# The third mixer of a fused four-layer block, with its state-space groups started earlier

## The reference

```python
def odd_mixer(h, pos, w_in, lam_re, ..., q_norm, w_uq, kv_norm, w_ukv, w_out):
    u, c_q, c_kv, k_rope = split_cols(h @ w_in, ODD_SIZES)
    y_c = s5_group(u, ...)          # state space, 512 channels
    y_d = mla_group(c_q, c_kv, k_rope, pos, ...)   # latent attention, 8 heads
    return jnp.concatenate([y_c, y_d], axis=-1) @ w_out

def s5_group(u, ...):
    bu = jnp.einsum('bsgh,gph->bsgp', ug.astype(jnp.complex64), b_bar)
    _, state = lax.associative_scan(s5_combine, (a_el, bu), axis=1)
    y = jnp.real(jnp.einsum('bsgp,ghp->bsgh', state, cm)) + d_skip * ug
    y = jax.nn.gelu(y)
    return y * jax.nn.sigmoid(y @ w_glu + b_glu)

def mla_group(...):
    q = (rms_norm_2(c_q, q_norm) @ w_uq)     # nope and rope parts of the queries
    kv = (rms_norm_2(c_kv, kv_norm) @ w_ukv) # keys and values
    ...                                       # rope, causal softmax by blocks, values
```

## Time and profile before

| | us |
|---|---|
| median of 3 runs | 2521.75 (2520.43 to 2522.57) |
| the profiled execution | 2520.07 |
| its span in the trace | 2518.3 |
| PE busy | 2442.2 (97% of the span) |
| DVE busy | 1301.7 (52%) |
| POOL busy | 1059.2 (42%) |
| ACT busy | 866.6 (34%) |
| from the first matmul of the third mixer to its last | 1879.1 to 2139.0 |

### The profile page before, as it was taken

One profiled execution on the slowest core, in us unless ns is written; L12 is line 12 of the kernel. 1 busy time (PEld: TensorE's weight loads), 2 busy tenths in 40 slices (PEclk: granted clock), 3 DMA queues, 4 the chain that ended last, 5 costly groups with the idle time before them and its releaser, 6 DMA issues.

```text
span 2518.3 us, 30094 instructions
## 1 busy us (share of the span) xinstructions
PE 2442.2 (97%) x11662; PEld 1962.8 (78%) x11662; DVE 1301.7 (52%) x1928; ACT 866.6 (34%) x1360; POOL 1059.2 (42%) x830
## 2 busy tenths in 40 slices
PE   8999999999999999999999999999999889999998
PEld 6877767888888888876777778888888657788886
DVE  6336687533533321494767754686126855533301
ACT  4453346222322222334445533222224453322221
POOL 4323344644544444353322245554454223544442
PEclk9999999999999999999999999999999989999999
DMA  4212122232323233222222223323231112222232
GB/s 148 68 59 78 55 78 90 95 101 92 105 93 100 94 96 96 93 85 66 74 67 75 72 75 107 98 94 98 92 100 55 28 34 81 91 92 101 91 98 80
DMA packets 65646, 213.58 MB, mean 85 GB/s; under 512 B 7904, under 2 KB 10208, under 8 KB 65376
## 3 DMA queue, kind: packets, MB, share of 16 engines
q1 hardware_dynamic: 64496, 208.30, 25.8%
q10 hardware_dynamic: 1008, 3.35, 0.4%
HBM read 205.33 MB, written 2.10 MB: 82 GB/s over the span
## 4 chain that ended last, share of the span: by engine, by line
PE 88%; DVE 9%; issue 1%; ACT 1%; DMA 0%; DVEq 0%; ACTq 0%; SPq 0%
PE ps L632 25%; PE ps L633 24%; PE ps L634 24%; PE ps L653 1%; DVE T L2175 1%; PE ps L654 1%; PE ps L655 1%; PE ps L982 1%; PE ps L959 1%; PE ps L749 1%; PE ps L995 1%; PE ps L740 1%; PE ps L774 1%; PE ps L827 1%; DVE A L1893 0%
## 5 line engine op out<-in xcount | busy, mean ns | idle before, releaser
L603 POOL TENSOR_TENSOR w_lo<-w_raw,w_hi 128x512 fp32r<-128x512 f32 (+4 forms) x822 | 1049.5, 1301 | 1420.6 <-ACT w_hi L1302 1420.5
L632 PE MATMUL ps<-H,w_hi 128*128 128x512 f32 x1880 | 754.7, 401 | 21.3 <-DVEq L1870 11.4
L634 PE MATMUL ps<-H,w_lo 128*128 128x512 f32 x1880 | 736.8, 392 | 0.0
L633 PE MATMUL ps<-H,w_hi 128*128 128x512 f32 x1880 | 736.3, 392 | 0.0
L1302 ACT CAST w_hi<-w_raw 128x1024 fp32r<-128x1024 f32 (+4 forms) x411 | 402.9, 984 | 519.4 <-DMA w_raw<-in_weights_dram 513.1
L632 PEld LDWEIGHTS ps<-H,w_hi 128*128 128x128 f32 x1880 | 355.5, 189 | 115.2 <-issue 25.8
L632 PE MATMUL ps<-split,w_hi 128*128 128x512 f32 x1034 | 411.5, 398 | 6.8 <-issue 3.3
L634 PEld LDWEIGHTS ps<-H,w_lo 128*128 128x128 f32 x1880 | 355.1, 189 | 75.1
L633 PEld LDWEIGHTS ps<-H,w_hi 128*128 128x128 f32 x1880 | 355.6, 189 | 73.1 <-issue 2.7
L633 PE MATMUL ps<-split,w_hi 128*128 128x512 f32 x1034 | 403.4, 390 | 0.0
L634 PE MATMUL ps<-split,w_lo 128*128 128x512 f32 x1034 | 403.4, 390 | 0.0
(11 more groups left out here) (403 smaller groups left out, 2369.3 us busy)
## 6 DMA issues: line engine op xcount, KB each, us to landing
w_raw<-in_weights_dram SPq DMA_DIRECT2D x323, 512.0 KB, 3.5
w_raw<-in_weights_dram SPq DMA_DIRECT2D x48, 448.0 KB, 3.3
w_raw<-in_weights_dram SPq DMA_DIRECT2D x22, 256.0 KB, 2.6
A<-A SPq DMA_DIRECT2D x64, 64.0 KB, 2.0
X<-in_xt_dram SPq DMA_DIRECT2D x4, 512.0 KB, 7.9
out_dram<-A SPq DMA_DIRECT2D x8, 256.0 KB, 2.1
w_raw<-in_weights_dram SPq DMA_DIRECT2D x12, 128.0 KB, 2.0
w_raw<-in_weights_dram SPq DMA_DIRECT2D x6, 192.0 KB, 2.3
```

What stands on the lines that cost most here:

```text
L603: sub = nc.gpsimd.tensor_tensor(w_lo[:, p % NS, c], w_raw[:, p % NS, c], w_hi[:, p % NS, c].bitcast(F32), ALU.subtract)
L632: mm_(ps[:, bank, :], r(wh), xh, start=(k == 0), stop=False)
L633: mm_(ps[:, bank, :], r(wh), xl, start=False, stop=False)
L634: mm = mm_(ps[:, bank, :], r(wl), xh, start=False, stop=(k == kt - 1))
```

## The change

The change rearranges the third mixer.

- The columns of `od_in` are packed in another order: query latents 0 to 2 as before, the first three u sections as tiles 3, 4 and 5, the key latents 6 and 7, the last u section 8, the rope key 9. `od_slot` becomes a table.
- The tables of sines for sections 0 and 1 are made during `down2`; the others reuse the same two buffers, after the state parts of sections 0 and 1.
- Two strided copies and the cast of the positions go from DVE to ACT.
- On PE the eight `turns_b` stand between the units of tile 4, and regrouping and inputs stand between the units and tiles of `od_in` 5 to 9.
- On DVE the four recurrences stand between the evictions of tiles 5 to 9, the latents and the rope.
- `regroup_in`, `inputs_of` and the norms get other banks, and waits for them; each section has its own buffers (`S5X`, `S5G`, `S5H`, `S5T`).
- The loop of attention no longer holds state-space work; it starts after all four `regroup`s. Its filling products are `glu` 0 to 2, `uk` 2, `glu` 3, `uk` 3, `uv` 1, `out3a`, by 0, twelve times 4, 3, 3, 2 units.

```diff
-        "od_in": np.concatenate([od[:, 512:1152]] + 4 * [od[:, 1152:]] + [od[:, :512]], axis=1),
+        "od_in": np.concatenate([od[:, 512:896], od[:, :384], od[:, 896:1152], od[:, 384:512]] + 4 * [od[:, 1152:]], axis=1),
...
+    + tiles_of("od_in") + tiles_of("uq") + tiles_of("uk", 0, 2) + tiles_of("uv", 0, 1)
+    + tiles_of("glu", 0, 3) + tiles_of("uk", 2, 3) + tiles_of("glu", 3) + tiles_of("uk", 3) + tiles_of("uv", 1)
...
-        MLA_FILL = (3, 3, 2, 2, 5, 6, 5, 0, 4, 4, 4, 4, 4, 4, 4, 4)
+        MLA_FILL = (0,) + (4,) * 12 + (3, 3, 2)
...  PE, input phase
+            for i, _ in enumerate(zip(units(("od_in", 4), HX), turns_b())):
+                if i == 5:
+                    regroup_in(0)
             pe.wait_ge(s_s5w, 8)
             inputs_of(0)
...
+            tile("od_in", 6, HX)
             regroup_in(2)
+            tile("od_in", 7, HX)
+            inputs_of(2)
+            now = units(("od_in", 8), HX)
+            run(now, 4)
+            pe.wait_ge(s_buf, 2)
+            norm_cols("ckv", 7)
+            run(now, 8)
+            now = units(("od_in", 9), HX)
+            run(now, 3)
+            regroup_in(3)
+            norm_spread("ckv")
+            run(now, 8)
             pe.wait_ge(s_mq, 3)
             tile("uq", 0, QC)
-            regroup_in(3)
+            inputs_of(3)
             rotate_mla(0)
...  DVE
+            run(first, 2)
+            od(5)
+            copy_rms("cq", RQ, 5)
             run(first, 1)
+            od(6)
+            run(second, 2)
+            od(7)
+            run(second, 1)
+            add_square("ckv", 1)
+            latents(QC, 0, OD[:, 4, :], vec("od_q_norm", 0), RQ)
+            od(8)
+            run(third, 1)
+            for k in (1, 2):
+                latents(QC, k, OD[:, 4 + k, :], vec("od_q_norm", k), RQ)
+            rms("ckv")
+            run(third, 2)
+            dve.wait_ge(s_sin, 2)
+            cosine(COSM)
+            od(9)
+            copy_rms("ckv", RK)
             rope_mla(0)
+            run(fourth, 1)
             rope_mla(1)
-            recurrence(1)
+            run(fourth, 1)
             rope_mla(2)
-            recurrence(2)
-            last = recurrence_parts(3)
-            run(last, 1)
+            run(fourth, 1)
+            for k in range(2):
+                latents(KC, k, OD[:, 7 + k, :], vec("od_kv_norm", k), RK)
...  ACT, before the loop of attention
+            gelu(3)
+            values(0)
+            hi_to(last_panel("uv", 0) + 5)
+            halve(2)
             nc.scalar.preload_act_table_set("exp_and_others")
-            hi_to(last_panel("uv", 0) + 5)
+            halve(3)
```

More of the change, by code:

```diff
@@ L1241, in fill_mla @@
             def fill_mla():
-                for t in (1, 2, 3):
-                    yield from units(("uk", t), KC)
+                pe.wait_ge(s_yg, 4)
+                for t in range(3):
+                    yield from units(("glu", t), YG)
+                yield from units(("uk", 2), KC)
+                yield from units(("glu", 3), YG)
+                yield from units(("uk", 3), KC)
                 yield from token_units(("uv", 1), KC)
-                pe.wait_ge(s_yg, 4)
-                for t in range(4):
-                    yield from units(("glu", t), YG)
                 pe.wait_ge(s_yc, 4)
@@ L1257, in _ @@
                 run(fill, n // 2)
-                if s == 1:
-                    outputs_of(3)
-                if s == 2:
-                    regroup(3)
                 pe.wait_ge(s_pn, 32 + s + 1)
@@ L1479, in _, with ffn @@
             x_squares("out1", "ffn1")
-            def ffn(k, after, beside=None):
+            def ffn(k, after, beside=None, beside_down=None):
                 norm = f"ffn{k}"
@@ L1677, in sines, with turns, first_tables @@
                 A_(cs, cs, ACT.Identity, scale=-2.0, bias=con("ones")[:, 0:1]).then_inc(s_tabx, 1)
+            def turns(s):
+                for t in range(4 * s, 4 * s + 4):
+                    turn = A_(TURNS[s][:, CH * (t % 4):CH * (t % 4) + CH], lvec("time", 0, CH), ACT.Copy,
+                              scale=s5[:, 2, t:t + 1])
+                turn.then_inc(s_turn, 1)
+            def first_tables(t):
+                if t == 1:
+                    act.wait_ge(s_s5p, 2)
+                    turns(0)
+                    turns(1)
+                if t == 3:
+                    sines(0)
+                    sines(1)
+            ffn(2, "mix3", s5_scales, first_tables)
+            act.dma_start(POSM.bitcast(I32), positions.to_broadcast([P, S])).then_inc(s_pos, 16)
             def col(name):
                 return lvec(name, 0, 256).rearrange("p (t c) -> p t c", t=16)
-            act.wait_ge(s_s5p, 2)
+            act.wait_ge(s_s5z, 1)
+            for half in range(2):
+                rows = slice(64 * half, 64 * half + 64)
+                for c in range(2):
+                    spread = nc.scalar.copy(BW[rows, c].rearrange("p t (j h n) -> p t j h n", j=TAPS, h=2)[:, :, :, half, :],
+                                            BB[rows, c])
+            spread.then_inc(s_s5b, 1)
             hi_to(last_panel("od_in", 0) + 4)
@@ L1700, in _, with copy_b @@
             act.wait_ge(s_s5c, 2)
[L1702 to L1710 removed]
+            def copy_b(i):
+                b = (0, 4, 1, 5, 2, 6, 3, 7)[i]
+                act.wait_ge(s_s5t, i + 1)
+                nc.scalar.copy(A[:, BW_AT + 512 * b:BW_AT + 512 * b + 512], ps[:, 5 + i % 2, :]).then_inc(s_s5w, 1)
             def copy_in(m):
                 act.wait_ge(s_regrouped, m + 1)
[L1714 removed]
+                nc.scalar.copy(UU[:, 4 * m:4 * m + 4, :], four(ps[:, U_BANK[m], :])).then_inc(s_gs, 1)
             def square_od(n, k, t):
                 act.wait_ge(s_od, t + 1)
[L1718 to L1721 removed]
+                square(n, k, OD[:, od_slot[t], :])
+            turns(2)
+            turns(3)
             hi_to(last_panel("od_in", 3) + 4)
@@ L2132, in _, with ffn @@
             add_to_x("out1", "ffn1", lambda k: ("norm_ffn", k))
-            def ffn(k, after, gain, beside=None):
+            def ffn(k, after, gain, beside=None, beside_down=None):
                 norm = f"ffn{k}"
@@ L2618, in _ @@
             mla_maxima(0)
-            run(last, 1)
+            for m in range(1, 4):
+                split_gelu(m)
             mla_maxima(1)
```

327 lines of the change are left out of this document (142 added, 185 removed).

## The result

The changed kernel took 2528.54 us (median of 9 runs, 2525.58 to 2530.35), the kernel before 2520.43 in the same comparison (9 runs, 2518.54 to 2523.03). The ratio, estimated from the runs of both kernels and not simply the quotient of the two medians (1.0032), is 1.0026, 95% interval 1.0017 to 1.0034: slower by a quarter of a per cent. The forecast was 2519.4 with a range up to 2528.

The account below looks back on a forecast made before the run. PE bounds it, busy 97% of the span, with DVE ending last in the input phase. 7.1 us earlier at full clock, less 4.8 for the clock, leaves 2.3: 2521.75 - 2.3 = 2519.4 us, range 2511 to 2528.

Parts of the forecast that it names:

- DVE's wait at the rotation: Input phase, before DVE's three rope parts: DVE waits 2.4 us for PE's `inputs_of(3)` and the rotation.
- DVE's chain to the key latents: Before `uk` 0: three rope parts 7.2, a recurrence 12.1 (range 12.1 to 12.7), two key latents 4.4; 23.7 us.
- the clock paragraph: Input phase to loop: new PE waits lower its clock, costing 4.8 us; the spreading's share falls into the `inputs_of(3)` wait.
- E + 15.9: When the column sum in tile 8 can start; E is the end of `od_in` tile 6, at 1941.5 us.
- The clock on tile 8: Behind the 3.8 us column sum wait: lowered clock costs up to 2.5 us on tile 8, taken as 1.8.
- From `uk` 0 to the scores of step 2: Stretch ahead of the loop: 19.7 us including PE waits of 2.2 and 2.7, plus 3 for the clock.
- The loop: Attention loop up to `out3b`: 103.2 us of work plus 0.9 of waiting at step 1.
- None of the waits of rows 3 lies in them: Attention loop: the earlier kernel's steps 9 to 15, also with four filling units, held none of its listed PE waits.
- slower, about 2530: Rival, chance 0.13: three input-phase waits keep PE at 0.50 clock through `uq`, deciding once PE needs over DVE's 23.7 us; +9.
- No change: The forecast's own case, chance 0.46: old waits go, same-sized ones come in the input phase; 2517 to 2525 us.
- The early tables stay beside `down2`: Sine tables of sections 0 and 1 on ACT, counted 0; rival that they do not, chance 0.07, 2522.4 us.
- this gives PE nothing: Strided copies moved to ACT: DVE gets 7.5 us ahead, then waits for `od_in` 3 as before; no gain for PE.

Follow-up runs that it names:

- spare matmuls: Changed kernel plus unread matmuls where PE waited; ahead of `uk` 0, `regroup(3)` and the first transposes (last three places) 2525.00 us; at all five places 2526.17 us.
- keys ahead: Changed kernel; column sum behind tile 8, rotation before `inputs_of(3)`, DVE's norm reciprocal before two query latents, key latents before the fourth "out" part: 2519.13 us.
- eviction 9: The fastest kernel with DVE's eviction of tile 9 ahead of the second and third parts of section 2's recurrence: 2516.02 us, ratio 0.9975.
- the fastest kernel: The "keys ahead" kernel plus halving copies before the values' copies on ACT and three `glu` units before the first transposes: 2512.97 us, ratio 0.9973.

## Why the prediction was wrong

The waits and what causes them were right, and terms of the sum were wrong in size: DVE's wait at the rotation (2.4 us forecast, 3.06 measured), DVE's chain to the key latents (23.7 and 25.3), the loop (104.1 and 106.7) and the clock (1.8 and 3 forecast, 2.6 and about 4 measured). Every wait of the forecast is in the trace, released by the engine named: 3.8 us forecast and 4.3 measured at the column sum, 6.3 and 6.0 at the spreading, 2.3 and 2.8 ahead of `uk` 0, 2.2 and 2.0 at `regroup(3)`, 2.7 and 1.8 at the transposes. Only at `inputs_of(3)` it was 1.3 and not 4.1, as the clock paragraph had it: PE came late through its low clock. The column sum was foreseen at E + 15.9 = 1957.4 and began at 1957.48. The forecast then had `out3b` over 2.3 us sooner than in the kernel before, at 2136.7; it was over at 2143.48. These are the 6.8 us, in five steps:

1. **The clock on tile 8**: 1.8 in the sum, 2.6 measured (tile 8 foreseen at 1961.1 with a full clock; DVE's eviction begins at 1963.95, 0.25 behind it). The four units of tile 8 cost the 1.8; the column sum itself also runs at half clock, which I left out. +0.8.
2. **`inputs_of(3)` and the rotation**: DVE waits 3.06 and not 2.4 us. +0.7.
3. **DVE's chain to the key latents**, 23.7 forecast, 1987.65 to 2012.98 = 25.3 measured. +1.6. I took prices from rows where GpSimd stood aside. In the fourth "scan" (3.6 us and not 3.1), the fourth "out" part (5.3 and not 4.5) and the first key latent it did not; two of DVE's rows, then GpSimd's:

```profile
2005.16 1.12 DVE L2583 TENSOR_TENSOR H<-H,T 128x512 f32<-128x512 f32 x1
2006.31 1.11 DVE L2584 TENSOR_TENSOR H<-H,T 128x512 f32<-128x512 f32 x1
```

```profile
2004.76 2.11 POOL L607 TENSOR_TENSOR w_lo<-w_raw,w_hi 128x256 fp32r<-128x256 f32 x2 [3.96 <-ACT w_hi L1315]
2008.03 1.87 POOL L607 TENSOR_TENSOR w_lo<-w_raw,w_hi 128x256 fp32r<-128x256 f32 x2 [1.16 <-ACT w_hi L1315]
```

   Each of DVE's rows is 0.69 alone. "I take the lower" end of 12.1 to 12.7 was the wrong choice; the higher end came from the same kind of collision.
4. **From `uk` 0 to the scores of step 2**: 19.7 + 3 for the clock forecast, 2013.10 to 2036.79 = 23.7 measured. +1.0. The spare matmuls confirm that this is clock, and size it: with those at the last three places this part takes 19.5 us (2016.38 to 2035.91), where the sum without the clock had 19.7. So the clock costs about 4 us here, where the sum had 3. The load of the table took the 1.28 us of the row, and the halving copy behind it began after 0.41 us more, in which it waited for PE.
5. **The loop**: 103.2 + 0.9 = 104.1 forecast, 2036.79 to 2143.48 = 106.7 measured. +2.6. With the spare matmuls at the last three places the loop has its full clock, and its window shows the work apart from the waits:

```profile
2035.90:2142.40 106.50, 103.35 (x552) 1.00 0.21 64
```

   Work is 103.35 us, where I had 103.2. The miss is in the waits: 3.2 us in that kernel (1.0 for the issue of a tile, 0.9 for the probabilities, 0.8 and 0.5 for ACT) and not 0.9. In the changed kernel itself they are 2.5, and the other 0.8 is the clock at the loop's start. "None of the waits of rows 3 lies in them" was true of the long ones; I took the short ones out with the 8.7 us of idle time and did not put them back.

These five make 6.7. The forecast of the time missed by 9.1 us, and the other 2.3 stay open. 1.3 of them are those behind `out3b`. The last 1.0 is the distance of the median from the profiled execution: I took 1.7, and it is 2.7 in the changed kernel, whose profiled execution has a mean granted clock of 0.990 and whose slower runs show 0.987 to 0.988. In the kernel before, the profiled execution lies 0.4 us under the median of the same comparison. So a part of the result is clock that no trace of mine locates; that `inputs_of(0)` begins up to 5.9 us apart in the traces shows that such differences also arise ahead of the mixer.

Of the prediction's own signs, the five waits came, and none for the states of section 2 or 3. But `uk` 0 came at 2013.10 and not at 2008 to 2011, and two signs of being wrong came with it: DVE stood idle 4.58 and 3.06 us between 1943 and 2008, together more than the 5 named, and the loop has four waits of 0.3 to 1.0 us.

Of the rivals, "slower, about 2530" has the number and not the mechanism. It wanted `uq` at half clock; the window from 1985 to 2010 is at 1.00. Its deciding point, PE needing more than DVE's time up to the key latents, was not reached. "No change" failed by little: from 1911 to 2139 PE waits 21.5 us and not 19.5, and loses 0.06 x 206.5 = 12.4 us to the clock and not 10.4; these 4.0 are about the 4.5 by which `out3b` ends later. The early tables stay beside `down2`, as forecast: PE begins the tap products at 1897.02, in the kernel before at 1898.04.

The price of the strided copies, "this gives PE nothing", I would not repeat. Putting them back cost a wait of 2.9 us at the mixer's first norm, although in the kernel before they caused none; whether they do hangs on a memset of GpSimd, which began 1.1 us behind their end in the kernel before and inside the last of them here.

What I did not ask is where the larger lever lay: I said that DVE is what ends last in the input phase and then counted its waits for PE (tile 8, the rotation) as given. The stretch of "keys ahead" shows that they were the choice of the lists: the same instructions in another order, 11.6 us.

## What to carry to other kernels

Where two in-order engines feed each other, look in each list for what stands directly behind an instruction that waits for the other engine. If the other engine needs it next, the wait is paid twice: moving one column sum behind four units, and one rotation ahead of one step, brought `uk` 0 forward by 2.9 and 1.9 us as single edits. A wait that only the later engine causes is handed on when it is removed (eviction 9); shortening that engine's way to the result (the key latents ahead of a part nobody waits for) is what pays.

Price a short wait of TensorE by what is queued behind it. Ahead of work on the critical path three waits of 2 to 3 us cost 4.3 us more through the clock, which filling them with unused matmuls gave back; where TensorE waited again anyway, filling gave nothing.

## What the runs showed of the hardware

A short DVE instruction can be held for a whole memset of GpSimd. In the changed kernel this scaling takes 4.85 us where a like one takes 0.43:

```profile
1892.86 4.85 DVE L2266 TENSOR_SCALAR A<-A 128x512 f32<-128x512 f32 x1
1897.75 0.43 DVE L2267 TENSOR_SCALAR A<-A 128x512 f32<-128x512 f32 x1
```

```profile
1891.26 2.73 POOL L607 TENSOR_TENSOR w_lo<-w_raw,w_hi 128x512 fp32r<-128x512 f32 x2
1893.92 3.52 POOL L615 MEMSET A<- 128x4096 f32 x1
```

It began inside GpSimd's splitting and ended 0.27 us behind the memset's end at 1897.44. The last of the strided copies, 5.11 us instead of 1.67, ended 0.5 us behind the same memset. The Trainium skill (SBUF — State Buffer, "Who interferes with whom") says that a DVE scaling or copy in a two-port mode and a GpSimd instruction need the same pair of ports, and that whoever issues first holds it for its whole instruction while the other is blocked. The trace agrees with that in the ends of both rows; whether these instructions ran in such a mode, no row says.

The granted clock can fall behind single waits of about 2 to 3 us in work that is otherwise dense. In the changed kernel it is 0.50 in 2030 to 2035, behind waits of 2.0 and 1.8 us; with seven unused matmuls in each of these waits it is 1.00. It does not fall every time: with the keys ahead, the same wait of 2.0 us at `regroup(3)` left it at 1.00 from 2020 to 2025, and it fell (0.67 from 2025 to 2030) only behind the next wait, of 2.5 us. The time of a run follows its mean granted clock with the same kernel: the fastest kernel's runs took 2510.94 us at 0.995, 2514.01 at 0.992 and 2519.16 at 0.990.
